# Forget gate steps that keep their filling, and an opening whose norm weight row is spread by a product with ones

## The chip, the cores and the metric

The kernel runs on one core of one Trainium2 chip. The metric is the device time of one execution in microseconds (us). TensorE (PE in the profile, PEld for its weight loads) multiplies, ScalarE (ACT) and VectorE (DVE) work on its results, GpSimd (POOL) does a few small operations and one kind of DMA, and SyncE (SP) issues nearly all DMAs.

## The reference, cut to what matters

`x` is 256 rows of 1024 numbers. Two layers of a first block come first (the change lies in them), then two layers of a second block (feed forward, mixing, cross attention, feed forward), which the change doesn't touch.

```python
def first_block(x, pre_norm, post_norm, w_in, ...):
    for layer in range(DEPTH):                      # 2
        h = rmsnorm(x, pre_norm[layer])
        proj = h @ w_in[layer]
        (hq, hf, hi, hz, nq, kc, vc, ks, vs, kw, vw, ng, nz) = jnp.split(proj, offsets, axis=-1)
        o_h = hgrn2_mixer(heads(hq), heads(hf), heads(hi), lower_bounds[layer]...)
        o_h = rmsnorm(o_h, ...) * jax.nn.silu(hz)
        o_n = nsa_mixer(...) * jax.nn.silu(nz)
        y = jnp.concatenate([o_h, o_n], axis=-1) @ w_out[layer]
        x = x + rmsnorm(y, post_norm[layer])
    return x
```

`hf` is the forget gate: its log sigmoid (in layer 1 with a lower bound) is summed along each chunk of 64 rows.

## The kernel before, in words

**Numbers in two parts.** A product of 32-bit numbers is made from three products of rounded parts: each weight piece (128x2048, 1 MB) is split by ACT into a high part (`split_high`, L2261) and by DVE into a low part (`split_low`, L2477). The activations are turned by TensorE (`turn`, L2023), then split by ACT (`turn_split`, L2278) and DVE (L2501). `tok` (L1968, L1972 for the weight's high part, L1978 for its low part) multiplies one weight piece with one tile of 128 rows, 12 products of 512 columns. `ch` (L1992, L1995, L1998) does 128 output columns of one piece for both tiles, 12 products of 256 columns.

**The plan.** A Python planner (`make_plan`) writes one list of steps, and each engine runs those that are its own in the order of the list. An engine's queue is strictly in order, so a step that waits holds back all behind it on its engine.

**Opening.** SP issues `load_ident`, `load_x` of tile 0, weight piece p0, `load_x` of tile 1, p1, p2, 17 small loads, p3, the constants, p4, p5 and `load_swap`. POOL issues a DMA (`gpre`, L2987) that copies the norm's weight row, 4 KB, to all 128 partitions, 512 KB. Both tiles are normed (`norm_squares` on ACT L2350, `norm_mean` on DVE L2565, `rstd` on POOL L2965, `norm_scale` on DVE L2573). The plan's order (`begin`, seam without `yb`) is: square tile 0, scale it, split_high p0, square tile 1, turn tile 0, both turn_splits of tile 0, scale tile 1, then the splits of p1, p2, p3 with their low parts. `mm_halves` then runs tile 0 over p0, p1, p2, p3, and then tile 1 over the same four: eight `tok`, tile 1 turned ahead of the fourth. A piece's slot comes free with its tile 1 product. `gT` is a small table of turned weights that `setup` (L1936) fills after the eight `tok`.

**The spread.** In each layer of the first block, `spread(plan, main, side)` mixes main steps (compress, the two attention groups `nsa(0)`, `nsa(1)`, and `recurrence`, one step of each in turn by `both`) with filling from `projections` and `out_early`, which is weight products for TensorE. After each main step the variable `ahead` falls by `plan.pace` (2.0, from the queries on 1.0, from the end of attention on 2.2) times 2400 units of planned TensorE work, and the side runs until it is positive again. A `ch` counts 3072 units, which is 1.28 paces of 2400; a `tok` counts 2.56. The second heads' projection `hgrn_qf(1)` runs inside this filling. It alternates eight `ch` of the query with the gate's steps (`softplus` on ACT for each half, `forget` on DVE for each half, L2742 to L2752, in layer 1 `bounded` L2758 to L2763, then `decay` L2770 and `log_key`: ACT L2425, DVE L2777), through `both`. Each gate step but the last cluster ends in `yield "rest"`, and at a rest `spread` stops filling and sets `ahead = 0`. The main steps beside it are those of attention: `scores` (PE L2032, DVE L2540 to L2547), `soft_exp` (ACT L2326), `nsa_gate` (DVE L2725 to L2730), `keys` (PE L2040, copied by ACT L2335 or DVE L2554) and `pv` (PE L2049). The first heads' `hgrn_qf(0)` runs outside `spread`, with nothing between; after it come `same` (PE L2130) and the level steps (L2141, L2152, L2805, L2812).

```python
            if step == "rest":
                ahead = 0
        yield
```

Of the kernel before, what the change touches and what calls it, by code (L numbers as in the profile page):

```python
# [12 lines left out]
ALU = mybir.AluOpType  # L13
# [3 lines left out]
P = 128  # L17
# [129 lines left out]
class Signals:  # L147


    def __init__(self, sem):  # L150
# [21 lines left out]
        self.x = [sem(f"s_x{t}") for t in range(2)]  # L172
# [159 lines left out]
def spread(plan, main, side):  # L332

    live, ahead = True, 0
    for more in main:
# [38 lines left out]
class Plan:  # L374
# [37 lines left out]
    def later(self, us, part):  # L412

        self.lag.append((self.work + us * 2400, part))
# [181 lines left out]
    def turn_pairs(self, name, src, need, h, t, scal=None, gains=None):  # L596
# [5 lines left out]
        for q, bank in enumerate(banks):  # L602
            self.split_bank(name, q, bank, h.pairs[q], t, ("turnp", name, q), scal,
                            None if gains is None else gains[:, 4 * q:4 * q + 4])
            h.made(t, q, name)

# [96 lines left out]
class Seam:  # L703
# [3 lines left out]
    def __init__(self, plan, name, gain_rows, yb=None, gsrc=None, half=False, norm=True):  # L707
# [4 lines left out]
        if norm:  # L712
# [3 lines left out]
    def turn_row(self, t):  # L716
# [3 lines left out]
        self.plan.turn_pairs(name, tmp.ap, [[("row", f"{self.name}.n{t}", i)] for i in range(2)], self.h, t)  # L720
        self.plan.U.give(tmp, ("turnp", name, 1))

    def steps(self, t):
# [17 lines left out]
        if self.norm:  # L741
            for self.row[t] in plan.norm(nn, x, plan.x_made[t], ("gpre", self.name), plan.m.gpre[:, :]):
                yield
# [43 lines left out]
def begin(plan, seam, make_jobs):  # L787
    if seam.yb is None:
        plan.split_next(True)
        steps = seam.steps(1)  # L790
        next(steps)
        seam.turn_row(0)
        for _ in steps:
            pass
        plan.hold = False
        plan.pump()
    else:
        if seam.h is None:
            seam.turn_row(0)
        seam.turn(1)  # L800
    plan.lead = LEAD
    jobs = make_jobs()
    yield from plan.mm_halves(jobs, seam.h, lambda: seam.turn_row(1))
# [3 lines left out]
def make_plan(A, m, order):  # L807
# [9 lines left out]
    plan.x_made = [[("x_in", t)] * 2 for t in range(2)]  # L817
    plan.gpost_used = plan.gpre_used = None
    do("load_ident")
    do("load_x", t=0, dst=plan.xt[0].ap)  # L820
# [72 lines left out]
    def first_layer(l, seam):  # L893
        w_in, w_out = A["w_in"][l], A["w_out"][l]
        N = f"a{l}"
        def jobs():
            return [(f"{N}.kv{br}", plan.weight(w_in, 0, 8, c0, 512), [B.take(), B.take()])
                    for br, c0 in enumerate((5632, 6144))]

        made = []  # L900
        h = yield from begin(plan, seam, lambda: made.extend(jobs()) or made)
        if l == 0:
            setup()
# [244 lines left out]
        def hgrn_qf(hg):  # L1148
# [5 lines left out]
            made_q, key = [], []  # L1154

            def gate_f():
                t2 = bounds = None
                if l == 1:
                    t2 = U.take()
                    bounds = [a[:, 4 * hg:4 * hg + 4] for a in (LNLB, LN1M, NEG_LNLB)]  # L1160
                yield "rest"
                for q, (b, pr) in enumerate(fb):
                    do("softplus", name=H, q=q, need=pr, bank=b, tl=tl, t2=t2, bounds=bounds)
                    yield "rest"
                for q, (b, pr) in enumerate(fb):
                    do("forget", name=H, q=q, bank=b, k_=k_, tl=tl, tc=tc, bounds=bounds)
                    B.give(b, ("logf", H, q))
                    yield "rest"
                if l == 1:
                    do("bounded", name=H, k_=k_, tl=tl, tc=tc, t2=t2, bounds=bounds)  # L1170
                    U.give(t2, ("bounded", H))
                do("decay", name=H, bb=bb, tc=tc, need=("bounded", H) if l else ("logf", H, 1))
                U.give(tl, ("decay", H))
                U.give(tc, ("decay", H))
                kk = U.take()
                do("log_key", name=H, sp=k_, kk=kk, bb=bb, need=("sp_bounded", H) if l else ("softplus_f", H, 1))
                key.append(kk)

            def query():
                for q, (b, pr) in enumerate((yield from proj_ch(f"{H}.q", 512 * hg, 512))):  # L1180
                    made_q.append(plan.copy(f"{H}.q{q}", [pr], q_.ap[:, q * 512:q * 512 + 512], b.ap, "act",
                                            q_.after))
                    B.give(b, made_q[-1])

# [1952 lines left out]
```

## Time and profile before

| | us |
|---|---|
| median of 3 runs | 2163.52 (2162.01 to 2165.08) |
| profiled execution, its own time | 2163.67 |
| its span in the trace | 2161.9 |
| TensorE busy | 2103.6 |
| VectorE busy | 1418.8 |
| ScalarE busy | 1051.7 |
| GpSimd busy | 110.1 |

The profiled execution lies 0.15 us above the median, and 1.8 us of its time lie outside the span. A view of the trace is read as start (us from the span's start), duration, engine, line of the kernel, what is written and read, and in brackets how long the engine stood idle before it and what ended that.

### The profile page before, as it was taken

The page shows a single profiled execution, that of the slowest core. Times are in us where ns is not written, and L with a number is a line of the kernel's source. Part 1 is how long each engine was busy: PE and PEld are TensorE (multiplying, and loading weights), DVE is VectorE, ACT ScalarE, POOL GpSimd, SP SyncE. Part 2 cuts the span into 40 slices and gives each one's busy share as a digit, 9 for nine tenths or more (in the row PEclk, how much of TensorE's full clock was granted, in tenths as well). Part 3 has the DMA queues.
Part 4 walks back from the last instruction along what each step waited for, and adds up shares of the span by engine and source line. Part 5 has one row for each costly group of instructions (what it writes and reads, how often), then busy time and mean ns, then how long its engine had stood idle before and what let it go on. Part 6 is the DMA issues. An engine that isn't in the chain of part 4 may idle for free.

```text
span 2161.9 us, 27716 instructions
## 1 busy us (share of the span) xinstructions
PE 2103.6 (97%) x11555; PEld 1804.1 (83%) x11555; DVE 1418.8 (66%) x1802; ACT 1051.7 (49%) x1520; POOL 110.1 (5%) x121
## 2 busy tenths in 40 slices
PE   7999999999899999999999999999999999999998
PEld 6989887988787888787888888888888878888887
DVE  4657866747777766665775666576666666755665
ACT  5444545534544644544544455455545454454543
POOL 0100200100011100000000000000100000000000
PEclk9999999999999999999999999999999999999999
DMA  7453235353234765445455455565645445554552
GB/s 278 121 196 118 84 131 176 121 191 130 78 130 150 243 208 172 150 148 165 169 185 183 136 196 189 184 212 184 214 149 180 138 160 173 192 175 147 180 191 98
DMA packets 193125, 357.76 MB, mean 165 GB/s; under 512 B 8364, under 2 KB 85352, under 8 KB 193000
## 3 DMA queue, kind: packets, MB, share of 16 engines
q1 hardware_dynamic: 190120, 345.51, 47.9%
q0 software_dynamic: 2880, 10.49, 1.5%
q8 instruction: 91, 1.49, 0.3%
q14 instruction: 34, 0.28, 0.0%
HBM read 354.92 MB, written 1.05 MB: 165 GB/s over the span
## 4 chain that ended last, share of the span: by engine, by line
PE 87%; DVE 8%; ACT 2%; issue 1%; DMA 1%; POOL 0%; DVEq 0%; SPq 0%; ACTq 0%
PE bank L1972 16%; PE bank L1978 16%; PE bank L1968 16%; PE bank L2010 12%; PE bank L2014 6%; DVE raw_r L2477 3%; PE bank L2032 3%; PE bank L2049 2%; PE bank L2152 2%; PE bank L2023 2%; PE bank L1992 2%; PE bank L1995 2%; PE bank L1998 2%; PE bank L2070 1%; PE bank L2040 1%
## 5 line engine op out<-in xcount | busy, mean ns | idle before, releaser
L2477 DVE TENSOR_TENSOR raw_r<-raw,high 128x2048 fp32r<-128x2048 f32 x304 | 686.3, 2272 | 84.4 <-ACT high L2261 83.3
L2261 ACT ACTIVATE high<-raw 128x2048 fp32r<-128x2048 f32 x304 | 575.1, 1896 | 246.5 <-PE bank L1978 195.9
L1968 PE MATMUL bank<-high,units_r 128*128 128x512 f32 (+1 forms) x1576 | 630.8, 400 | 7.0 <-ACT units_r L2278 7.0
L1972 PE MATMUL bank<-high,units_r 128*128 128x512 f32 (+1 forms) x1576 | 618.7, 393 | 14.7 <-DVE units_r L2501 12.0
L1978 PE MATMUL bank<-raw_r,units_r 128*128 128x512 f32 (+1 forms) x1576 | 424.6, 390 | 4.0 <-DVE raw_r L2477 4.0
L1972 PEld LDWEIGHTS bank<-high,units_r 128*128 128x128 f32 x1576 | 297.8, 189 | 79.7 <-DVE units_r L2501 16.5
L1968 PEld LDWEIGHTS bank<-high,units_r 128*128 128x128 f32 x1576 | 297.9, 189 | 69.0 <-issue 10.8
L1978 PEld LDWEIGHTS bank<-raw_r,units_r 128*128 128x128 f32 x1576 | 296.5, 188 | 68.1 <-DVE raw_r L2477 6.4
L2010 PE MATMUL bank<-units_r,high 128*128 128x512 f32 x1152 | 288.2, 392 | 0.3 <-DVE units L2833 0.3
L2010 PEld LDWEIGHTS bank<-units_r,high 128*128 128x128 f32 x1152 | 208.4, 189 | 38.7 <-issue 0.6
L2014 PEld LDWEIGHTS bank<-units_r,raw_r 128*128 128x128 f32 x1152 | 157.2, 190 | 11.2
L2014 PE MATMUL bank<-units_r,raw_r 128*128 128x256 f32 x1152 | 160.6, 282 | 0.0
L2833 DVE TENSOR_TENSOR units<-bank,units 128x256 f32<-128x256 f32 x144 | 60.3, 421 | 151.2 <-ACT units L2294 151.2
L2965 POOL TENSOR_TENSOR stat<-stat,halfs 128x1 f32<-128x1 f32 (+2 forms) x64 | 52.7, 825 | 1708.2 <-DVE stat L2586 895.8
L2294 ACT ACTIVATE units<-bank 128x256 f32<-128x256 f32 x144 | 54.2, 376 | 170.2 <-PE bank L2014 170.2
L2326 ACT ACTIVATE units<-units,stat 128x256 f32<-128x256 f32 (+2 forms) x176 | 74.0, 422 | 117.9 <-DVE stat L2547 117.6
L2278 ACT ACTIVATE units_r<-bank 128x512 fp32r<-128x512 f32 x92 | 49.7, 595 | 141.0 <-PE bank L2023 107.2
L1992 PE MATMUL bank<-units_r,high 128*128 128x256 f32 x448 | 117.2, 293 | 0.0
L1995 PE MATMUL bank<-units_r,high 128*128 128x256 f32 x448 | 114.0, 286 | 0.0
L2501 DVE TENSOR_TENSOR units_r<-bank,units_r 128x512 fp32r<-128x512 f32 x84 | 53.9, 684 | 55.8 <-ACT units_r L2278 55.8
L1995 PEld LDWEIGHTS bank<-units_r,high 128*128 128x128 f32 x448 | 87.4, 195 | 0.4
L1992 PEld LDWEIGHTS bank<-units_r,high 128*128 128x128 f32 x448 | 87.4, 195 | 0.5
(258 smaller groups left out, 2213.5 us busy)
## 6 DMA issues: line engine op xcount, KB each, us to landing
raw<-in_ffn_w_dram SPq DMA_DIRECT2D x132, 1024.0 KB, 5.1
raw<-in_w_in_dram SPq DMA_DIRECT2D x108, 1024.0 KB, 5.1
raw<-in_w_out_dram SPq DMA_DIRECT2D x24, 1024.0 KB, 4.9
raw<-in_cross_wkv_dram SPq DMA_DIRECT2D x16, 1024.0 KB, 5.1
raw<-in_w_branch_dram SPq DMA_DIRECT2D x12, 1024.0 KB, 4.9
raw<-in_cross_wq_dram SPq DMA_DIRECT2D x8, 1024.0 KB, 5.1
raw<-in_cross_wo_dram SPq DMA_DIRECT2D x8, 1024.0 KB, 4.8
raw<-in_w_in_dram SPq DMA_DIRECT2D x4, 832.0 KB, 4.6
```

The source lines that it names most:

```text
L1968: pe.matmul(o, h.high(k0 + k)[:, span], p.hi[k][:, cols], start=start and k == 0, stop=False, skip_group_check=True)
L1972: pe.matmul(o, h.low(k0 + k)[:, span], p.hi[k][:, cols], start=False, stop=False, skip_group_check=True)
L1978: product = pe.matmul(o, h.high(k0 + k)[:, span], p.lo[k][:, cols], start=False, stop=stop and k == p.k - 1, skip_group_check=True)
L1992: pe.matmul(o, w, h.high(k0 + k), start=first and k == 0 and c % 2 == 0, stop=False, skip_group_check=True)
L1995: pe.matmul(o, w, h.low(k0 + k), start=False, stop=False, skip_group_check=True)
L2010: pe.matmul(bank.ap.rearrange("p (a s) -> p a s", a=2), p.hi[k][:, c * P:c * P + P], h.whole(k, m.units_r), start=k == 0, stop=False, skip ...
L2014: product = pe.matmul(bank.ap[:, 0:256], p.lo[k][:, c * P:c * P + P], h.high(k), start=False, stop=k == p.k - 1, skip_group_check=True)
L2032: score = pe.matmul(bank.ap[:, i * L:i * L + L], left, right, start=j == 0, stop=j == steps - 1, skip_group_check=True)
L2261: done = act.activation(high, raw, ACT.Copy)
L2326: done = act.activation(p3[:, h, :], p3[:, h, :], ACT.Exp, bias=mx[:, h:h + 1], scale=1.0, accum_out=sm[:, h:h + 1])
L2477: done = dve.tensor_tensor(low, raw, high.bitcast(F32), ALU.subtract)
L2833: dve.tensor_tensor(dst, bank.ap[:, 0:256], dst, ALU.add).then_inc(*mark(s.vout, ("folded", name, c)))
```

## The change

**Filling.** In `spread` a rest now ends the filling after this main step, and `ahead` keeps its value. In `hgrn_qf` the gate's steps become nine (layer 0: six) single parts, each followed by a rest: `bounded` is cut into three phases, and `decay` and `log_key` each stand alone. The query's copies no longer wait for the end of the gate's list, and whichever comes last, key or query, makes the result known to the recurrence. `later` inserts by due time.

**Opening.** The weight row is fetched by SP in front of all else, 4 KB to one partition. POOL sets a row of ones, and two TensorE products (one row by 512 columns) spread it over 128 partitions into two PSUM banks, from which `norm_scale` of both tiles reads it. The POOL DMA of 512 KB is gone. x is loaded by halves, four DMAs with a semaphore each, and tile 0 of x now stands ahead of the identity. In the plan, tile 0 is turned, its first half split, then p0 split high and low, then its second half split, then tile 1 normed. Then each piece is used with both tiles before the next: p0 tile 0, turn tile 1, p1 tile 0, p0 tile 1, p1 tile 1, then p2 and p3 likewise.

```diff
-            if step == "rest":
-                ahead = 0
+            if step == "rest":
+                break
...
     if seam.yb is None:
-        plan.split_next(True)
-        steps = seam.steps(1)
-        next(steps)
-        seam.turn_row(0)
-        for _ in steps:
-            pass
-        plan.hold = False
-        plan.pump()
+        def first_piece():
+            plan.split_next(True)
+            plan.low_next()
+
+        seam.turn_row(0, first_piece)
+        for _ in seam.steps(1):
+            pass
+        plan.lead = LEAD
+        for i, (name, w, banks) in enumerate(make_jobs()):
+            for t in range(2):
+                for pi, (k0, p) in enumerate(w):
+                    if i == t == 0 and pi == len(w) - 1:
+                        seam.turn_row(1)
+                        plan.hold = False
+                    plan.tok(name, p, t, [banks[t]], seam.h, k0, pi == 0, pi == len(w) - 1)
+                    yield
+        return seam.h
...
+    do("load_gain", src=gain_rows.pop(0))
+    do("load_x", t=0, dst=plan.xt[0].ap)
     do("load_ident")
-    do("load_x", t=0, dst=plan.xt[0].ap)
...
+            parts = [(softplus, 0), (softplus, 1), (forget, 0), (forget, 1)]
+            parts += [(bounded, phase) for phase in range(3)] if l else []
+            parts += [(decay,), (log_key,)]
+
+            def gate_f():
+                yield "rest"
+                for part, *how in parts:
+                    part(*how)
+                    yield "rest"
...
+    def gain_row(banks, **_):
+        hold.wait_ge(*at(("ones",)))
+        hold.wait_ge(*at(("gain_in",)))
+        for i, b in enumerate(banks):
+            pe.matmul(b.ap, m.gT[0:1, 0:P], m.gpre[0:1, i * 512:i * 512 + 512], start=True, stop=True,
+                      skip_group_check=True).then_inc(*mark(s.turned, ("gain_row", i)))
+        hold.wait_ge(*at(("ident",)))
...
+    pool.memset(m.gT[0:1, 0:P], 1.0).then_inc(*mark(s.pstep, ("ones",)))
...
     def load_x(t, dst, **_):
-        sp.dma_start(dst, A["x"][0, t * P:(t + 1) * P, :]).then_inc(*mark(s.x[t], ("x_in", t), by=16))
+        for i in range(2):
+            sl = slice(i * 512, i * 512 + 512)
+            sp.dma_start(dst[:, sl], A["x"][0, t * P:(t + 1) * P, sl]).then_inc(
+                *mark(s.x[2 * t + i], ("x_in", t, i), by=16))
+
+    def load_gain(src, **_):
+        sp.dma_start(m.gpre[0:1, :], src).then_inc(*mark(s.gain, ("gain_in",), by=16))
```

## Rows read from the trace of the kernel before

**Rows 1.** Waits of TensorE over the span: engine line, releaser: us, times, longest.
```profile
PE bank L1972 <- DVE units_r L2501: 12.0, 11, 2.5
PE bank L2023 <- DVE units L2573: 8.3, 1, 8.3
```

**Rows 2.** Timeline of the opening, from the landing of x to the first products.
```profile
4.88 0.63 ACT L2350 ACTIVATE units<-units 128x512 f32<-128x512 f32 x1 [2.85 <-DMA units<-in_x_dram]
...
7.43 1.42 DVE L2573 SCALAR_TENSOR_TENSOR units<-units,stat,gpre 128x512 f32<-128x512 f32 x2 [1.02 <-DMA gpre<-in_pre_norm_dram]
...
8.32 1.94 PE L2023 MATMUL bank<-consts,units 128*128 128x128 f32 x8 [8.32 <-DVE units L2573]
...
9.71 1.91 ACT L2261 ACTIVATE high<-raw 128x2048 fp32r<-128x2048 f32 x1 [3.50 <-DMA raw<-in_w_in_dram]
...
12.75 1.06 ACT L2278 ACTIVATE units_r<-bank 128x512 fp32r<-128x512 f32 x2
...
13.47 0.77 PE L1968 MATMUL bank<-high,units_r 128*128 128x512 f32 x1 [3.21 <-ACT units_r L2278]
13.71 1.91 ACT L2261 ACTIVATE high<-raw 128x2048 fp32r<-128x2048 f32 x1
...
15.12 0.63 PE L1972 MATMUL bank<-high,units_r 128*128 128x512 f32 x1
...
15.38 1.41 DVE L2573 SCALAR_TENSOR_TENSOR units<-units,stat,gpre 128x512 f32<-128x512 f32 x2 [0.67 <-POOL stat L2965]
...
16.71 8.89 DVE L2477 TENSOR_TENSOR raw_r<-raw,high 128x2048 fp32r<-128x2048 f32 x4
...
19.05 2.08 PE L1978 MATMUL bank<-raw_r,units_r 128*128 128x512 f32 x4 [1.60 <-DVE raw_r L2477]
...
22.53 0.39 PE L1968 MATMUL bank<-high,units_r 128*128 128x512 f32 x1
```

**Rows 3.** Window: length, busy of PE, PEld, DVE, ACT, POOL; clock; DMA share, GB/s.
```profile
8.00:10.00 2.00, 1.68 (x8) 1.57 (x8) 0.84 (x2) 0.29 (x1) 0.00 (x0) 1.00 1.04 414
```

**Rows 4.** Chain of waits, start and duration: ends of two `tok`, `setup`, ends of two `ch`.
```profile
35.42 0.91 PE bank L1978 x4
38.14 0.91 PE bank L1978 x4
...
42.08 0.26 PE bank L1936
...
46.17 0.48 PE bank L1998 x4
47.61 0.48 PE bank L1998 x4
```

**Rows 5.** Timeline: `keys` behind the gate's steps, layer 0.
```profile
234.80 1.97 PE L2040 MATMUL bank<-consts,units 128*128 128x128 f32 x8 [3.54 <-DVE units L2730]
```

**Rows 6.** The same in layer 1.
```profile
565.16 1.97 PE L2040 MATMUL bank<-consts,units 128*128 128x128 f32 x8 [3.73 <-DVE units L2730]
...
581.12 2.41 PE L2049 MATMUL bank<-units 128*128 128x128 f32 x14 [2.97 <-DVE units L2554]
```

**Rows 7.** Windows behind the gaps, columns as in rows 3.
```profile
238.00:240.00 2.00, 2.00 (x12) 2.00 (x11) 1.93 (x5) 0.64 (x1) 0.00 (x0) 0.50 0.00 0
240.00:242.00 2.00, 2.00 (x16) 2.00 (x16) 1.97 (x2) 0.00 (x0) 0.00 (x0) 0.79 0.00 0
...
568.00:569.00 1.00, 1.00 (x8) 1.00 (x8) 1.00 (x3) 0.00 (x0) 0.00 (x0) 0.73 0.00 0
...
1234.00:1236.00 2.00, 2.00 (x7) 1.54 (x6) 1.90 (x5) 0.00 (x0) 0.55 (x1) 0.53 0.70 238
...
1972.00:1974.00 2.00, 1.67 (x7) 1.42 (x8) 2.00 (x5) 0.00 (x0) 0.39 (x1) 1.00 1.04 361
```

**Rows 8.** Timeline after the first heads' gate, layer 1: key, then `same`.
```profile
391.27 1.04 ACT L2425 ACTIVATE units<-units 128x1024 f32<-128x1024 f32 x1
...
395.49 2.05 PE L2130 MATMUL bank<-units 128*128 128x128 f32 x16 [0.69 <-ACT units L2288]
```

More of the change, by code:

```diff
@@ L170, in __init__ @@
         self.pstep = sem("s_pstep")
-        self.x = [sem(f"s_x{t}") for t in range(2)]
+        self.x = [sem(f"s_x{i}") for i in range(4)]
+        self.gain = sem("s_gain")
         self.const = sem("s_const")
@@ L412, in later @@
     def later(self, us, part):
-        self.lag.append((self.work + us * 2400, part))
+        at = self.work + us * 2400
+        i = sum(due <= at for due, _ in self.lag)
+        self.lag.insert(i, (at, part))
     def due(self, all_=False):
@@ L605, in turn_pairs @@
             h.made(t, q, name)
+            if between and q == 0:
+                between()
     def split_bank(self, name, q, bank, pair, t, need, scal=None, gains=None):
@@ L711, in __init__, with turn_row @@
             plan.do("gpost", name=name, src=gsrc, used=plan.gpost_used)
-        if norm:
+        self.gain = gain
+        if norm and not gain:
             plan.do("gpre", name=name, src=gain_rows.pop(0), used=plan.gpre_used)
         self.h = None
-    def turn_row(self, t):
+    def turn_row(self, t, between=None):
         if t == 0:
@@ L719, in turn_row @@
         tmp, name = self.row[t], f"{self.name}.h{t}"
-        self.plan.turn_pairs(name, tmp.ap, [[("row", f"{self.name}.n{t}", i)] for i in range(2)], self.h, t)
+        self.plan.turn_pairs(name, tmp.ap, [[("row", f"{self.name}.n{t}", i)] for i in range(2)], self.h, t,
+                             between=between)
         self.plan.U.give(tmp, ("turnp", name, 1))
@@ L741, in steps @@
         if self.norm:
-            for self.row[t] in plan.norm(nn, x, plan.x_made[t], ("gpre", self.name), plan.m.gpre[:, :]):
+            for self.row[t] in plan.norm(nn, x, plan.x_made[t], *(self.gain or ([("gpre", self.name)] * 2, plan.gpre))):
                 yield
@@ L895, in first_layer @@
         N = f"a{l}"
+        made = []
         def jobs():
[L897 to L901, printed above, removed]
+            for br, c0 in enumerate((5632, 6144)):
+                made.append((f"{N}.kv{br}", plan.weight(w_in, 0, 8, c0, 512), [B.take(), B.take()]))
+                yield made[-1]
+        h = yield from begin(plan, seam, jobs)
         if l == 0:
+            for b in g_banks:
+                B.give(b, ("row", "in.n1", 1))
             setup()
@@ L1154, in hgrn_qf, with softplus, forget, bounded @@
             made_q, key = [], []
[L1156 to L1170, printed above, removed]
+            t2 = bounds = None
+            if l == 1:
+                t2 = U.take()
+                bounds = [a[:, 4 * hg:4 * hg + 4] for a in (LNLB, LN1M, NEG_LNLB)]
+            def softplus(q):
+                do("softplus", name=H, q=q, need=fb[q][1], bank=fb[q][0], tl=tl, t2=t2, bounds=bounds)
+            def forget(q):
+                do("forget", name=H, q=q, bank=fb[q][0], k_=k_, tl=tl, tc=tc, bounds=bounds)
+                B.give(fb[q][0], ("logf", H, q))
+            def bounded(phase):
+                do("bounded", phase=phase, name=H, k_=k_, tl=tl, tc=tc, t2=t2, bounds=bounds)
+                if phase == 2:
                     U.give(t2, ("bounded", H))
+            def decay():
                 do("decay", name=H, bb=bb, tc=tc, need=("bounded", H) if l else ("logf", H, 1))
@@ L1177, in gate_f, with ready @@
                 key.append(kk)
+                ready()
+            def ready():
+                if key and len(made_q) == 2:
+                    st_["qf", hg] = (q_, k_, bb, key[0], made_q[-1], ("key", H), ("log_key", H))
             def query():
@@ L1906, in drive @@
                 return e.value
-    seam = Seam(plan, "in", gain_rows)
+    g_banks = [B.take(), B.take()]
+    do("gain_row", banks=g_banks)
+    seam = Seam(plan, "in", gain_rows, gain=([("gain_row", i) for i in range(2)], [b.ap for b in g_banks]))
     seam.turn(0)
```

50 lines of the change are left out of this document (27 added, 23 removed).

## The prediction

> **What bounds the kernel now.** I read the waits of TensorE first. It is busy for 2103.6 of 2161.9 us, so 58.3 us is all that an order of work can win, and the reader is to see how few waits make up much of it: 8.3 us in one piece ahead of the first turn and 12.0 us in eleven small ones [rows 1], and 7.3 us in two pieces ahead of `keys` [rows 5, 6]. The eleven lie nearly all at the seams, which the change leaves alone. The other two lie where the change works, so I read two timelines next, the opening and the stretch beside the gate's steps, and then the granted clock behind each gap.
>
> **Opening, what is on the path.** The time up to `setup` at 42.08 [rows 4] is made of a late start and a slow start. Tile 0 is squared from 4.88, and its scaling starts at 7.43, after a wait of 1.02 whose last releaser is the copied weight row [rows 2]. The turns end at 10.26. Their halves are split only at 12.75, because ACT's queue has split_high p0 (9.71 to 11.62, held by the weight's landing) and the squares of tile 1 in front. The first product starts at 13.47, and a 1.60 gap waits for p0's low part, which DVE does only from 16.71, behind the scaling of tile 1 [rows 2]. A product of 512 columns takes 0.63 at 15.12 and 0.39 at 22.53 [rows 2]. The granted clock reads 1.00 here all the while, but the durations show the lower level, 1.2 GHz, in the first stretch: 0.43 from product to product (512 columns at 1.2 GHz), against 2.72 for twelve, so 0.23, later [rows 4].
>
> **Opening, step by step after.** The weight row (4 KB) and half of x go first. POOL's 512 KB DMA is gone; its row of ones is one more tiny operation ahead of nothing. SP has three more issues (weight row, two second halves), so p0 and all behind it are issued later; no row here prices one, and I take 1 us for the three at most. The transfers queue up behind each other anyway, and half a megabyte less stands in them. The two spreading products run while x is still on its way; no row shows one, they lie between nothing (hidden before 4.88) and 1.7 us, twice the cold spacing of a 512-column product with a second pass, and even that ends before the turns. I take nothing.
> Scaling then starts at about 6.8 (between 6.2, all of the wait of 1.02 and a little of the squares saved by the first half of x, and 7.4 as now). The first turn is done about 1.9 us later at 8.7, its ACT half (0.53) at 9.2. Split_high p0 starts there if p0 has landed; it landed by 9.71 with the 512 KB beside it, and at the 414 GB/s of 8 to 10 us [rows 3] that much is 1.3 us, so 8.4 to 9.7. It ends at 11.1 (11.6 at the late end), and `tok` of p0 and tile 0, which needs only the first half and p0, starts there. DVE makes p0's low part (8.89 for four, so 2.2) right behind, at 13.3, before its products are due. Cold, twelve products at 0.43 end at 16.2. Tile 1: squares behind the second half's split, 11.7 to 13.0, mean and rstd 0.8 (before, 0.67 of DVE's wait for POOL and the mean), scaling 1.41, so 15.3; its turns fit behind 16.2 and take 1.0 warm, 1.9 cold. At 17.2 seven `tok` are left at 2.72 each [rows 4], 19.0 us, so `setup` comes at 36.2 instead of 42.08. Each piece now feeds TensorE for 5.4 us against 2.2 of DVE and 1.9 of ACT, so no split is late; p1 must be split by 17.2, and ACT took it up at 13.71 even before [rows 2]. The gain is 5.9. Bounds: 3.4 (p0 as late as now and the turns and one `tok` still cold) to 7.0.
>
> The Trainium skill, page "DMA: Bandwidth & Descriptors", "Anatomy of one DMA", speaks against halves: a DMA costs about 2.0 us fixed and then its bytes at 436 GB/s. By it a half of x issued at 1.66 lands at about 4.3, no later than the whole at 4.88 in the trace, so its fixed part hides behind the first half and the sum stays.
>
> **Filling, what the gaps are.** In layer 0 `keys` waits 3.54 us for DVE's `nsa_gate` [rows 5]. DVE has attention's scores, then a `forget`, and only then this `nsa_gate`; TensorE has one `ch` beside all that. In layer 1 the same place waits 3.73, and `pv` 16 us later waits 2.97 for a copy on DVE behind `bounded`, `decay` and `log_key` in one block [rows 6]. Each of these gaps lets the clock fall. In layer 0 it is at 0.50, the 1.2 GHz level, at 238 to 240 and ends within 240 to 242 (0.79, so at 240.8); the eight products of `keys` at 234.80 took 1.97, so it was low from there [rows 5, 7]: 6 us of half work, 3.0 lost. Behind 565.16 it ends at about 568.5 (0.73), 3.3 us, so 1.6 lost. Behind 581.12 I take the same 1.6; no row here is given for it, and 0 and 3.0 bound it.
>
> **Filling, step by step after.** A `ch` leaves `ahead` at +0.28 paces, the next main step at -0.72, and the gate step's rest wipes that out. Four such rests and a small one lose 2.9 paces of filling per layer, and a `ch` comes only every second main step. After the change the debt stays and each main step gets a gate step and a `ch`. Walking the list: between `scores` and the waiting `keys` there are now two `ch`, not one. DVE's order there (scores, forget, nsa_gate) is as before, since `forget` of the second half moves in front of `nsa_gate` where that of the first half was. So the gap is 3.54 less 1.44, the spacing of two `ch` [rows 4], 2.1 us; in layer 1 3.73 less 1.44, 2.3. In layer 1 the block on DVE is cut, two `tok` (5.4 us) come between `keys` and `pv`, and I find 0.4 left of 2.97, so 2.6 gained. Sum of gaps: 1.44 + 1.44 + 2.6 = 5.5.
> Costs: `log_key` of layer 1's first heads now stands behind the query's copies, so `same`, which waits 0.69 for these, waits for the key of 1.04 too [rows 8]: 1.0. The second heads' level steps now follow `keys` at one place without filling, 0.7, and near the end of layer 1 one level step loses its `tok`, 0.5. Together 2.2, bounds 0 and 5. Net of gaps 3.3.
> Clock: the two longest seam gaps, 2.5 each [rows 1], one ahead of 1233.6 and one ahead of 1972.3, tell what 2.1 and 2.3 may do. Behind the first the clock fell (0.53), behind the second it did not (1.00) [rows 7]; behind 2.97 and more it fell each time. I give 2.1 and 2.3 a chance of one third, and 0.4 none: 2.0 + 1.1 + 1.6 = 4.7, less a little, 4.4. Bounds 0 to 6.2.
> The Trainium skill, page "TensorE: Matmul & The Clock Gate", "HAM oscillation", says that too long an idle stretch throttles TensorE again, and its "Part 1" that the watch over it runs free of the program. By that rule, the pair at 2.5 agrees.
> These two gaps, shifted in time, may fall or not anew. The shift at the seams is worth 1.6 either way for each of the two; it stands in the range.
>
> **Is the pulled-forward filling missed later?** The walk says no. The second heads start four main steps earlier in layer 0 and three in layer 1, so fewer of their steps fall after attention's end, where a step draws 2.2 paces and not 1.0. That saves about the 2.9 paces that are no longer lost. The filling ends at the same main step as before, ahead of the last `hgrn_v`.
>
> **Sum.** 2163.67 of the profiled execution (0.15 above the median, which I drop) less 5.9, 3.3 and 4.4 is 2150.1.
>
> **Rivals.** (A) The opening works, the gate's gaps don't close: DVE is the engine that ends last there, a moved split_low (2.2) slips in front of `nsa_gate`, and the gaps and the low clock stay. 2163.67 - 5.9 + 0.5 = 2158. For it: in layer 1 DVE is nearly full beside the gate; against: my walk has the split ahead of the scores. (B) The gate works, the opening doesn't: p0 or p1 lands as late as now and all is late behind ACT. 3.4 or less of the opening, so 2154 to 2156. (C) Slower: the filling drawn early is missed in the level steps, where each step without a `tok` shows a chain of DVE, ACT and DVE of about 2.5 us. It decides the sign when four steps in each layer stand bare (20 us, against 13.6), and gives 2170. Against it: the walk ends the filling at the same step. (D) The change does nothing that can be seen: the opening's gain is given back by a wait for the constants or the small loads at `setup`, and (A) too. 2162.
>
> **How the numbers follow.** Forecast 0.63, A 0.17, B 0.11, C 0.04, D 0.05. Within 0.2% means 4.3 us, about what a measurement can tell, so above 2159.3 counts as the same; a quarter of A reaches there. Faster 0.87, same 0.09, slower 0.04. The range runs from 2144 (opening 7.0, clock kept everywhere, 6.2, costs near 1) to 2158, which takes in B and the better half of A.
>
> **What would show it.** `setup` (L1936) between 35 and 39; first L1968 at 11 and no wait of L1978 behind it; no POOL DMA of the weight row in the opening. Waits of L2040 on L2730 two at about 2.2, that of L2049 on L2554 under 1. Granted clock 1.00 around 235 and 575. `same` of layer 1 waiting 1.7 on ACT. I am wrong if the gaps at L2040 are over 3 or new waits on L2477 or L2812 over 2 us appear in the level steps.

## The result, and the profile after

| | before | after |
|---|---|---|
| median, us | 2163.14 (2162.01 to 2165.08, 4 runs) | 2150.53 (2149.81 to 2151.60, 4 runs) |
| span of the profiled execution | 2161.9 | 2148.2 |
| TensorE busy | 2103.6 | 2099.2 |
| VectorE, ScalarE, GpSimd busy | 1418.8, 1051.7, 110.1 | 1417.2, 1051.1, 102.2 |

The ratio is 0.9941, 95% interval 0.9924 to 0.9958: faster by 12.6 us. Forecast were 2150.1 and "faster", a gain of 13.6. The total is right to half a microsecond; three of its terms are not, and they cancel.

TensorE's waits in the changed kernel (engine, line, releaser: us, times, longest). The first row answers [rows 1], the second [rows 5, 6]; L2021, L2072, L2089, L2190 and L2179 are the old L1972, L2023, L2040, L2141 and L2130.

```profile
PE bank L2021 <- DVE units_r L2550: 12.1, 11, 2.5
PE bank L2089 <- DVE units L2779: 4.4, 2, 2.3
...
PE bank L2017 <- ACT high L2310: 2.9, 1, 2.9
...
PE bank L2190 <- DVE units L2865: 2.6, 2, 1.9
...
PE bank L1976 <- DMA gpre<-in_pre_norm_dram: 2.3, 1, 2.3
PE bank L2179 <- issue: 1.7, 1, 1.7
...
PE bank L2072 <- DVE units L2622: 1.3, 1, 1.3
```

The seams' 12 us stay. The 7.3 us ahead of `keys` are 4.4. New are 2.9 for the first piece, 1.9 ahead of `across` (L2190) and 1.7 ahead of `same` (L2179).

Timeline of the opening after, which answers [rows 2] (columns as there):

```profile
2.27 3.75 PE L1976 MATMUL bank<-gpre,gT 1*128 1x512 f32 x4 [2.27 <-DMA gpre<-in_pre_norm_dram]
...
4.22 0.63 ACT L2399 ACTIVATE units<-units 128x512 f32<-128x512 f32 x1 [2.19 <-DMA units<-in_x_dram]
...
6.45 1.41 DVE L2622 SCALAR_TENSOR_TENSOR units<-units,stat,bank 128x512 f32<-128x512 f32 x2 [0.68 <-POOL stat L3019]
...
7.34 1.94 PE L2072 MATMUL bank<-consts,units 128*128 128x128 f32 x8 [1.32 <-DVE units L2622]
8.46 0.60 ACT L2327 ACTIVATE units_r<-bank 128x512 fp32r<-128x512 f32 x1 [2.89 <-PE bank L2072]
...
10.27 1.91 ACT L2310 ACTIVATE high<-raw 128x2048 fp32r<-128x2048 f32 x1 [1.21 <-DMA raw<-in_w_in_dram]
...
12.23 0.80 PE L2017 MATMUL bank<-high,units_r 128*128 128x512 f32 x1 [2.95 <-ACT high L2310]
...
15.75 1.10 PE L2027 MATMUL bank<-raw_r,units_r 128*128 128x512 f32 x4
16.68 1.27 PE L2072 MATMUL bank<-consts,units 128*128 128x128 f32 x8
```

Squares, scaling and turns come earlier, as forecast. Then ScalarE, done with the turns' half, waits 1.21 for the first piece. That piece now ends last. By the chain of waits `setup` stands at 37.3 where it stood at 42.08 [rows 4].

The gaps after, in order of time: two `keys` (L2089), which answer [rows 5, 6], and between them `across` and `same`, the latter answering the wait in [rows 8].

```profile
231.41 1.09 PE L2089 MATMUL bank<-consts,units 128*128 128x128 f32 x8 [2.11 <-DVE units L2779]
...
257.03 1.14 PE L2190 MATMUL bank<-units 128*128 128x128 f32 x8 [1.85 <-DVE units L2865]
...
390.49 1.69 PE L2179 MATMUL bank<-units 128*128 128x128 f32 x13 [1.68 <-issue]
...
562.39 1.09 PE L2089 MATMUL bank<-consts,units 128*128 128x128 f32 x8 [2.30 <-DVE units L2779]
```

And the windows behind the first, second and fourth and behind the seam gap (columns as in rows 3; compare [rows 7]):

```profile
232.00:234.00 2.00, 2.00 (x19) 2.00 (x18) 1.97 (x2) 1.90 (x3) 0.00 (x0) 1.00 0.00 0
258.00:260.00 2.00, 2.00 (x12) 2.00 (x11) 0.09 (x1) 1.79 (x4) 1.10 (x1) 0.50 0.27 109
260.00:262.00 2.00, 2.00 (x11) 1.92 (x11) 0.39 (x1) 2.00 (x2) 0.34 (x1) 0.64 0.03 8
...
565.00:567.00 2.00, 2.00 (x20) 2.00 (x19) 1.93 (x5) 0.92 (x1) 0.00 (x0) 1.00 0.00 0
1222.00:1224.00 2.00, 2.00 (x10) 1.62 (x10) 1.90 (x5) 0.00 (x0) 0.55 (x1) 1.00 0.80 273
```

The clock stays at 1.00 behind 2.11 and 2.30 and behind the seam gap of 2.44, and falls to 0.50 behind 1.85, which is shorter than all three.

### The profile page after: what moved, and what is told of

Its sections match the earlier page's. It is cut to its first block, busy times and chain, and to the rows that moved or that the text cites. A ratio compares the mean times of both kernels' runs of the same rounds, so it can differ in the third digit from the quotient of the medians.

```text
span 2148.2 us, 27730 instructions
## 1 busy us (share of the span) xinstructions
PE 2099.2 (98%) x11559; PEld 1799.1 (84%) x11559; DVE 1417.2 (66%) x1801; ACT 1051.1 (49%) x1519; POOL 102.2 (5%) x121
## 3 DMA queue, kind: packets, MB, share of 16 engines
HBM read 354.40 MB, written 1.05 MB: 165 GB/s over the span
## 4 chain that ended last, share of the span: by engine, by line
PE 88%; DVE 7%; ACT 3%; DMA 1%; issue 1%; POOL 0%; SPq 0%; DVEq 0%; ACTq 0%
PE bank L2021 16%; PE bank L2017 16%; PE bank L2027 16%; PE bank L2059 12%; PE bank L2063 6%; PE bank L2081 3%; DVE raw_r L2526 3%; PE bank L2201 2%; PE bank L2047 2%; PE bank L2041 2%; PE bank L2044 2%; PE bank L2098 2%; PE bank L2072 2%; PE bank L2119 1%; PE bank L2089 1%; DMA raw<-in_w_in_dram 1%
## 5 line engine op out<-in xcount | busy, mean ns | idle before, releaser
L2526 DVE TENSOR_TENSOR raw_r<-raw,high 128x2048 fp32r<-128x2048 f32 (+1 forms) x305 | 689.6, 2275 | 84.3 <-ACT high L2310 83.2
L2310 ACT ACTIVATE high<-raw 128x2048 fp32r<-128x2048 f32 (+1 forms) x305 | 577.0, 1896 | 243.2 <-PE bank L2027 192.3
L2017 PE MATMUL bank<-high,units_r 128*128 128x512 f32 x1584 | 632.3, 399 | 6.9 <-ACT units_r L2327 3.9
L2021 PE MATMUL bank<-high,units_r 128*128 128x512 f32 x1584 | 619.9, 391 | 14.7 <-DVE units_r L2550 12.1
L2027 PE MATMUL bank<-raw_r,units_r 128*128 128x512 f32 x1584 | 425.2, 389 | 2.4 <-DVE raw_r L2526 2.4
L2021 PEld LDWEIGHTS bank<-high,units_r 128*128 128x128 f32 x1584 | 298.4, 188 | 79.3 <-DVE units_r L2550 16.2
L2041 PE MATMUL bank<-units_r,high 128*128 128x256 f32 x448 | 114.6, 288 | 0.0
L2044 PE MATMUL bank<-units_r,high 128*128 128x256 f32 x448 | 112.1, 283 | 0.0
```

Of the source, the lines that this page charges most:

```text
L2017: pe.matmul(o, h.high(k0 + k)[:, span], p.hi[k][:, cols], start=start and k == 0, stop=False, skip_group_check=True)
L2021: pe.matmul(o, h.low(k0 + k)[:, span], p.hi[k][:, cols], start=False, stop=False, skip_group_check=True)
L2027: product = pe.matmul(o, h.high(k0 + k)[:, span], p.lo[k][:, cols], start=False, stop=stop and k == p.k - 1, skip_group_check=True)
L2041: pe.matmul(o, w, h.high(k0 + k), start=first and k == 0 and c % 2 == 0, stop=False, skip_group_check=True)
L2044: pe.matmul(o, w, h.low(k0 + k), start=False, stop=False, skip_group_check=True)
L2310: done = act.activation(high, raw, ACT.Copy)
```

## The experiments

Each run's landmarks (us) tell where it gained: the first `same`, the first product behind layer 0's end, the same for layer 1, the product behind the seam gap of 2.4, and the span. The last column counts the gaps behind which the granted clock fell after the opening, without the fall at the very end that every trace has. Each row is one profiled execution; that of the opening alone is the slowest of its eight runs, that of the filling alone the slowest of its six.

| run | `same` | layer 0 end | layer 1 end | seam | span | falls |
|---|---|---|---|---|---|---|
| before | 66.05 | 327.23 | 661.25 | 1233.61 | 2161.9 | 4 |
| after | 61.30 | 321.23 | 649.17 | 1221.71 | 2148.2 | 1 |
| opening only | 62.35 | 323.24 | 657.30 | 1229.66 | 2157.8 | 4 |
| filling only | 66.20 | 327.95 | 656.98 | 1229.43 | 2156.0 | 3 |
| debt kept | 61.73 | 320.15 | 653.47 | 1225.87 | 2154.0 | 3 |
| steps cut | 61.80 | 321.74 | 656.66 | 1229.09 | 2155.7 | 3 |
| level_mul early | 62.07 | 317.07 | 644.65 | 1216.99 | 2143.5 | 0 |
| + later parts whole | 61.23 | 314.71 | 641.69 | 1213.97 | 2142.1 | 1 |
| identity by POOL | 60.48 | 318.58 | 647.25 | 1219.73 | 2147.8 | 2 |
| p1 behind p0 | 60.81 | 320.49 | 649.28 | 1221.85 | 2151.7 | 4 |
| half MB back | 62.38 | 323.74 | 651.44 | 1223.91 | 2150.4 | 2 |
| old piece order | 62.20 | 322.02 | 649.81 | 1222.35 | 2148.9 | 1 |
| x whole | 62.22 | 323.76 | 652.50 | 1225.02 | 2154.8 | 5 |
| all three | 60.99 | 314.82 | 642.20 | 1214.66 | 2142.8 | 1 |

### Each half of the change alone

The changed kernel with `spread` and `hgrn_qf` of before; `later` stays as changed:

```diff
             if step == "rest":
-                break
+                ahead = 0
...
-            parts = [(softplus, 0), (softplus, 1), (forget, 0), (forget, 1)]
```

> The changed kernel with the filling part undone (the gate's steps whole, the debt dropped at a rest). Theory (the two parts add up): setup still at about 37.3 us, 4.7 earlier than before; the gaps of keys near 230 and 560 are 3.5 and 3.7 again and that of pv near 576 is 3.0, each with the granted clock at 0.5 behind it; the wait of 1.85 at the second heads' first level step is gone back to about 0.7. By the difference of the two traces the filling is worth 1.3 us in layer 0 and 6.0 in layer 1, so the span is 2148.2 + 7.3 = 2155.5, plus 1.7 if the clock falls behind the seam gap near 1229, time about 2157 to 2159. Rival (the filling's gain is a matter of where the clock happens to fall, not of the gaps): the gaps are back but the clock behind them is at 1.00 in two of the three, and the span is 2152 or less.

Measured: 2157.26 (2155.34 to 2159.60), ratio 0.9977 (0.9966 to 0.9988). Its gaps are those of before again (3.55, 3.73, 3.01), each with the clock at 0.50 behind it, and `same` of layer 1 waits 0.69.

The kernel before with the changed `spread` and `hgrn_qf`; `later` and the opening are those of before. Part of its edit, against the changed kernel:

```diff
-    do("load_gain", src=gain_rows.pop(0))
-    do("load_x", t=0, dst=plan.xt[0].ap)
     do("load_ident")
+    do("load_x", t=0, dst=plan.xt[0].ap)
...
-        seam.turn_row(0, first_piece)
+        plan.split_next(True)
+        steps = seam.steps(1)
```

> The kernel before with only the filling part. Theory: setup at 42.1 as before, gaps of keys 2.1 and 2.3 with the clock at 1.00 behind them, no gap of 3 us at pv, the wait at the second heads' first level step in layer 0 at about 1.9. Span 2161.9 less 7.3, 2154.6, or 1.7 less where the seam gap near 1226 keeps its clock; time 2154 to 2156.5. Rival (the gap of 1.9 and its low clock in layer 0 came from the opening's shift): layer 0 then gains 3 us or more instead of 1.3.

Measured: 2156.15 (2154.79 to 2157.77), ratio 0.9970 (0.9959 to 0.9982), with the gaps of the changed kernel to the hundredth: 2.11, 1.85, 1.68, 2.30. The product of both ratios is 0.9947, against 0.9941 for both at once: the parts add up, and what `later` does on its own is not seen in either. Layer 0, from `same` to its end, takes 261.8 where it took 261.2, so it gains nothing without the opening's shift either, against the rival. But the clock behind equal gaps was another. Behind 2.11 it fell here, as these windows of this run show (columns as in rows 3), and it did not in the changed kernel:

```profile
238.00:240.00 2.00, 2.00 (x12) 2.00 (x11) 1.97 (x3) 2.00 (x2) 0.00 (x0) 0.50 0.00 0
240.00:242.00 2.00, 2.00 (x14) 2.00 (x14) 2.00 (x2) 0.70 (x2) 0.00 (x0) 0.70 0.00 0
```

### The filling's two edits apart

The debt is kept, but the gate's parts stay as they were, `bounded`, `decay` and `log_key` in one block, and the result again waits for both lists, key and query:

```diff
-            parts = [(softplus, 0), (softplus, 1), (forget, 0), (forget, 1)]
-            parts += [(bounded, phase) for phase in range(3)] if l else []
-            parts += [(decay,), (log_key,)]
+                if l == 1:
+                    do("bounded", name=H, k_=k_, tl=tl, tc=tc, t2=t2, bounds=bounds)
```

> The changed kernel, but the gate's steps stay whole (bounded, decay and log_key in one block); only the debt is kept at a rest. Theory: keeping the debt is what puts the second block of columns between scores and keys, so both gaps of keys are about 2.1 and 2.3 as in the changed kernel. What cutting the block buys is the gap at pv in layer 1: some of the 3.0 stays (1 to 3 us). Rival: the cut is what helps all three, and the gaps of keys are over 3.

Measured: 2155.78, one run. Both keys gaps fell below what I had expected, to 0.67 and 0.86, since three `ch` now stand between `scores` and `keys`. In layer 1 the block of `bounded`, `decay` and `log_key` stayed in one piece and a wait of 5.08, more than the 1 to 3 expected, stands at the `pv` right behind `keys`, one earlier than the one that waited 2.97 before (this run's timeline):

```profile
568.52 3.78 PE L2080 MATMUL bank<-units 128*128 128x128 f32 x16 [5.08 <-DVE units L2585]
```

The other way round, steps cut and debt dropped:

```diff
-                break
+                ahead = 0
```

> The changed kernel with its cut steps, but the debt dropped at each rest as before. Theory: only one block of columns stands between scores and keys, so the gaps of keys are about 3.5 and 3.7 again with the low clock behind them, and as there are more rests now more filling is lost; pv in layer 1 waits less than 3.0, since the block is cut. Span at least 4 us over the changed kernel's 2148.2. Rival: cutting alone closes the gaps, span within 2 us of 2148.2.

Measured: 2157.49, one run. The keys gaps are back at 3.55 and 3.73, the `pv` gap is gone, and a level step of layer 1 waits 2.01. The gap of 1.85 at `across` comes with the debt too: it stands in the run before and is 0.90 here. So the kept debt fills `keys` and the cut block frees `pv`; neither does the other's work. And the cut has a price that I had not seen: the rests that it adds, two in layer 0 and five in layer 1, eat up filling that the keys gap could have used (2.11 where 0.67 is to be had).

### The gap at `across`

```diff
             level_exp(0)
             level_from(1)
+            level_mul(0)
             yield
...
-                if li == 0:
-                    level_mul(0)
```

> The changed kernel with layer 0's level_mul emitted one main step earlier; nothing else differs. Theory (TensorE's new 1.85 us gap at `across` in layer 0 is the DVE queue: split_low, nsa_cat and the copy of keys stand in front of level_mul, 0.9 us late): with level_mul ahead of them the gap near 257 us falls to 0.5 or less, the granted clock stays at 1.00 behind it, and landmarks after it come 2.5 to 3.5 us earlier than in the changed kernel (seam gap 343.0 to about 340): span 2145 to 2146. Rival (the gap is the planner's order of PE work, the wait is ready only when the filling's copies are): the gap stays at 1.5 to 2, only its waited-on instruction changes, and the span stays within 0.5 us of 2148.2, or the copy of keys now comes 0.9 us later and the keys gap grows from 2.1 to 3.0 with the clock at 0.5 behind it: 2150.

Measured: 2145.53 (2145.32 to 2146.88), ratio 0.9924 (0.9909 to 0.9939). In the changed kernel DVE does a split_low, a step of attention and the copy of `keys` ahead of level_mul (L2865), and TensorE stands behind all of them (timeline of DVE):

```profile
250.95 2.29 DVE L2526 TENSOR_TENSOR raw_r<-raw,high 128x2048 fp32r<-128x2048 f32 x1
...
253.15 0.68 DVE L2784 TENSOR_TENSOR units<-bank,units 128x512 f32<-128x512 f32 x1
...
255.21 0.69 DVE L2603 COPY units<-bank 128x512 f32<-128x512 f32 x1 [1.38 <-PE bank L2089]
255.82 1.66 DVE L2865 TENSOR_TENSOR units<-units 128x512 f32<-128x512 f32 x2
```

With level_mul ahead of the split, `across` (here L2189) starts right behind `keys` (timeline of this run):

```profile
250.49 0.68 DVE L2864 TENSOR_TENSOR units<-units 128x512 f32<-128x512 f32 x1
...
251.09 2.28 DVE L2525 TENSOR_TENSOR raw_r<-raw,high 128x2048 fp32r<-128x2048 f32 x1
...
253.69 1.04 PE L2088 MATMUL bank<-consts,units 128*128 128x128 f32 x8
254.56 1.06 PE L2189 MATMUL bank<-units 128*128 128x128 f32 x8
```

The theory holds: from the first `keys` to the end of layer 0 it takes 86.1 where the changed kernel takes 89.8. Of these 3.7, the run with the identity on POOL, which has the gap of 1.85 but kept its clock behind it (88.2), gives 1.6 to the clock and 2.1 to the gap.

### The later parts of the gate without a rest

```diff
-                    yield "rest"
+                    yield "rest" if part in (softplus, forget) else 0
```

> As the run before it, and the forget gate's later parts (bounded, decay, log_key) keep DVE's block cut as in the change but no longer ask for the rest of a step's filling; only softplus and forget keep it. Theory (the keys gap of 2.1 and 2.3 us is one chunk of filling short, since the filling is eaten up by parts which need no cover): three chunks stand between scores and keys, so the two keys gaps are 0.7 and 0.9 us, no 3 us gap at the pv products, and the span is 2142 to 2145. Rival (what the later parts give up shows elsewhere: the filling ends later, so a DVE block stands in front of another tile): a gap of 2.5 us or more turns up at the pv products or in the level steps, clock at 0.5 behind it, and the span is 2147 to 2150.

This edit stands on top of the one before it. Measured: 2143.89 (2143.65 to 2145.10), ratio 0.9917 (0.9900 to 0.9933). Its timeline at the two `keys` and at `pv` (L2097):

```profile
230.07 1.09 PE L2088 MATMUL bank<-consts,units 128*128 128x128 f32 x8 [0.67 <-DVE units L2778]
...
555.51 1.09 PE L2088 MATMUL bank<-consts,units 128*128 128x128 f32 x8 [0.85 <-DVE units L2778]
...
571.16 1.83 PE L2097 MATMUL bank<-units 128*128 128x128 f32 x14 [0.64 <-DVE units L2602]
```

Both keys gaps are short and no long wait comes back at `pv`, as the theory had it. Up to the end of layer 1 it is 3.0 us ahead of the run before it, of which 0.84 were there at the first `same` and are not the edit's: 2.1 us are, less than the 2.9 by which the keys gaps shrank, since `pv` now waits 0.64. The seam gap then cost it the clock (0.50), which that run had kept, so the spans differ by 1.4.

### What sets the first piece's landing

The identity's DMA started by POOL:

```diff
-        sp.dma_start(m.consts[:, 0:P], A["consts"][:, 0:P])
+        pool.dma_start(m.consts[:, 0:P], src)
```

> The changed kernel with the identity's DMA started by POOL, so SP starts the first piece of x one issue (about 0.4 us) earlier: 2.1 where the changed kernel has 2.50. Theory (the first piece lands at 10.25 because it is issued 0.84 us later than before and shares the queues' bandwidth with what stands behind it): it lands 0.4 us earlier, at 9.8, ScalarE's split of it starts with it and the first token product at about 11.8 (12.23 in the changed kernel); span 2147.8. Rival (its landing is set by the bytes on the way, not by its issue): landing stays at 10.1 to 10.4, first token product at 12.2.

The second piece issued when the first has landed:

```diff
+        if p.i == 1:
+            hold.wait_ge(*at(("raw", 0)))
         sp.dma_start(dst, src)
```

> The changed kernel with SP waiting for the first piece's landing before it issues the second and what follows. Theory (the first piece's 7.7 us from issue to landing are stretched by the pieces behind it, which share the 16 DMA engines): it lands 1 us or more earlier, at 9.2 or before, the first token product starts at 11.2, and the second piece, issued at 9.2, lands 4 us or more later than in the changed kernel, so that TensorE waits 2 to 4 us at the second piece's products; span 2150 to 2152. Rival (pieces are served in the order they are issued, and those behind cost the first nothing): it lands at 10.0 to 10.4 as before, and only the later pieces are late: span 2151 to 2154.

The 512 KB of before given back, into a buffer that nobody reads yet:

```diff
+        pool.dma_start(m.gpost[:, :], src.partition_broadcast(P))
```

> The changed kernel with a 512 KB DMA given back: POOL copies the 4 KB row to 128 partitions of a buffer that is not used yet, as early as before; nobody waits for it in the opening. Theory of the prediction (the bytes stand in the queues ahead of the first piece, 512 KB at 414 GB/s are 1.3 us): ScalarE's split of the first piece starts at 11.5 where the changed kernel has 10.27, the first token product at 13.4 (12.23), setup at 38.5 (37.33). Rival (from the issue to the landing the first piece took 8.05 us with the 512 KB beside it and 7.77 without, so these bytes cost it 0.3 us): split at 10.4 to 10.7, first token product at 12.4 to 12.7, setup at 37.4 to 37.8.

x by whole tiles:

```diff
-        for i in range(2):
-            sp.dma_start(dst[:, sl], A["x"][0, t * P:(t + 1) * P, sl])
+        sp.dma_start(dst, A["x"][0, t * P:(t + 1) * P, :])
```

> The changed kernel with x loaded by whole tiles (two DMAs, not four), so the first piece is issued one issue (0.43 us) earlier, at 2.07. Theory (as in the run with the identity on POOL, what is issued ahead of the first piece delays it by its issue and a bit): ScalarE's split of it starts 0.4 to 0.8 earlier than 10.27, and since the squares of tile 0 start 0.2 to 0.6 later than 4.22 with cover to spare before that split, the first token product comes at 11.5 to 11.9 and setup at 36.5 to 36.9. Rival (halves pay by the early start of squares, scaling and turns): scaling starts at 7.1 or later (6.45 with halves), the ScalarE half of the turns ends after the piece's landing, and setup is at 37.3 or later.

Measured, one run each (2149.58, 2153.51, 2152.23 and 2156.60 us), from the timelines:

| run | scaling | p0 issued | split of p0 starts | first `tok` | products at 1.2 GHz until |
|---|---|---|---|---|---|
| after | 6.45 | 2.50 | 10.27 | 12.23 | about 15.5 |
| opening only | 6.35 | 2.50 | 10.29 | 12.26 | about 17.5 |
| identity by POOL | 6.92 | 2.03 | 9.43 | 11.38 | about 14.3 |
| p1 behind p0 | 6.23 | 2.51 | 9.67 | 11.63 | about 14.9 |
| half MB back | 8.21 | 2.51 | 10.72 | 12.68 | about 17.9 |
| x whole | 7.08 | 2.04 | 10.22 | 12.18 | about 17.5 |

The level is read from the products: 0.43 from one to the next is the lower one, 0.23 the higher, as in the prediction; the granted clock reads 1.00 throughout this stretch.

How much a single trace says here shows in the seven that load their opening alike, the changed kernel, the opening alone, debt kept, steps cut, level_mul early, later parts whole and the old piece order. In them p0 is issued at 2.50 or 2.51, but its split starts anywhere from 9.87 to 10.76, and the first `tok` from 11.83 to 12.72.

With x whole, p0 is issued 0.46 earlier and its split starts at 10.22, inside that range: no gain of the earlier issue is seen. Not issuing the second piece until the first has landed brings the split to 9.67, only 0.2 ahead of the earliest of the seven and less than the 1 us expected, so that what stands behind a transfer stretches it is not shown. The late second piece cost nothing (setup at 36.8), against theory and rival. Moving the 64 KB identity to POOL is the one edit that stands clear: the split starts at 9.43, and at 9.49 in the run with all three below, without any wait for the piece, 0.4 or more ahead of the earliest of the seven. Why 64 KB weigh that much isn't settled.

Half a megabyte given back hit x first, whose second half came late, by the timeline of that run:

```profile
6.61 0.63 ACT L2400 ACTIVATE units<-units 128x512 f32<-128x512 f32 x1 [1.51 <-DMA units<-in_x_dram]
```

Scaling starts 1.76 later, and of that 0.45 reaches the first `tok`, since TensorE waited for the piece anyway. The rival's split and first `tok` are right, its reason (bytes beside the piece) is not: the piece had landed by 10.72, when ScalarE came to it. `setup` comes at 38.4, later than the rival's 37.8, since the lower level lasted longer. Of the 1.3 us that I took off the piece's landing for these bytes at most 0.45 are there against the changed kernel, and at most 0.9 against the earliest of the seven.

Halves of x start the squares at 4.22, the whole at 4.88 as before [rows 2], which moves scaling by 0.63; none of it reaches the first `tok`. With x whole `setup` comes at 38.2, as the rival had it, but not for its reason: the turns' half ends at 9.70, ahead of the piece, and the lower level lasts until 17.5. The halves' second squares need no wait, so the second half had landed by 4.86, when the whole had. The Trainium skill, page "DMA: Bandwidth & Descriptors", "Anatomy of one DMA", gives each DMA that GpSimd issues a fixed part; x is issued by SyncE, but by that rule, as weighed in the prediction, the trace agrees: the second half, issued behind the first, was there at most 0.7 later, so its fixed part hid behind the first.

### The order of pieces alone

```diff
-        for i, (name, w, banks) in enumerate(make_jobs()):
-            for t in range(2):
+        plan.hold = False
+        plan.pump()
+        yield from plan.mm_halves(list(make_jobs()), seam.h, lambda: seam.turn_row(1))
```

> The changed kernel with its opening's products in the order of before: tile 0 over all four pieces, then tile 1. Theory (the pieces come slower than one tile eats them, 2.7 us a product warm, so each piece must feed both tiles): TensorE waits for the second to fourth piece's split or low part by 1 to 3 us in all, and setup comes at 38.5 to 40 where the changed kernel has 37.33. Rival (the earlier start alone makes the gain, the order is worth nothing): no wait over 0.5 us at the products of pieces two to four, setup at 37.0 to 37.8.

Measured: 2150.71, one run, setup at 38.2. One wait for the second piece's low part is nearly all that the old order costs (timeline of this run):

```profile
19.41 1.21 PE L2022 MATMUL bank<-raw_r,units_r 128*128 128x512 f32 x4 [0.74 <-DVE raw_r L2521]
```

`same` is 0.90 later than in the changed kernel, 0.74 of it this wait, with the clock up at the same place in both. (The other traces with this opening lie up to 1.05 later as well, but none has this wait.) It lies between theory and rival: the pieces keep pace but for the second.

### The best of it

Level_mul early, later parts whole, identity by POOL:

> The run with the later parts whole plus the identity on POOL: level_mul early, later parts of the gate without a rest, first piece issued earlier. Theory (the three add up): keys gaps of 0.7 and 0.9 us, no gap of 1.85 at `across`, setup at 36.4; span 2141.2, or 2139.6 if the clock stays up behind the seam gap of 2.4 near 1212, median 2142 to 2143.5. Rival (the earlier opening is given back, since the seams' waits and the clock's falls are luck of timing): span 2142 to 2145, no faster than the run without it (2142.1).

Measured: 2144.12 (2143.46 to 2144.55), ratio 0.9915 (0.9902 to 0.9929). No faster than without the identity's move (0.9917): the rival. The first `same` is 0.24 earlier, and by the first `keys` (230.17 against 230.07) this is given back, to a wait of 0.72 at L2200 near 149 that the other run does not have over 0.6. By the ratios both are some 5 us faster than the change itself, though the intervals overlap a little with its own (0.9924 to 0.9958).

## Why the prediction came out right

**Opening: right in mechanism, mis-sized in one term.** Forecast was a gain of 5.9, measured are 4.7 at `same`, and 3.7 to 4.8 in the six traces with this same opening. Scaling at 6.8 (6.45) and ScalarE's half done at 9.2 (9.06) held. SP's three more issues cost 1.34 at p1 where I took 1; the two of them ahead of p0 cost 0.84. The step that failed is the landing of p0, "8.4 to 9.7": it is 10.24, later than before, by the chain of waits after:

```profile
2.50 7.74 DMA raw<-in_w_in_dram
```

Before, the same chain has:

```profile
1.66 8.03 DMA raw<-in_w_in_dram
```

So the piece was issued 0.84 later and took 0.29 less: my working took 1.3 off the landing for the 512 KB and never added the later issue, which it had priced one sentence earlier. That moved the first `tok` from 11.1 to 12.23. A second term gave part of it back: I had all twelve first products at the lower level (5.1 us); the higher one came after eight (4.45). With the opening alone it did not, and `setup` stood at 38.4 instead of 37.3, which shows that this microsecond is the clock's and not the change's. The spreading products took 3.75 us where my bound was 1.7: each showed as two instructions. They were done at 6.02, only 0.4 ahead of scaling, which reads them and not the turns, and scaling waited for POOL, so nothing of it is on the path.

**Keys and pv: right.** The gaps of 2.1 and 2.3 are 2.11 and 2.30. For `pv`, 0.4 was forecast to be left of 2.97. Nothing is left at that `pv`, but another one, ahead of `keys`, which had no wait before, now waits 0.82 for ScalarE (at 553.18). 5.0 us gained where I had 5.5.

**Costs of the filling: one right, one missed.** `same` waits 1.68 (1.7 forecast). "0.7 at one place without filling" is 1.85, because I counted TensorE's missing filling and not what stands in DVE's queue: the walk followed the list for `nsa_gate`, but not for level_mul. A level step of layer 1 waits 0.75, but at the same place it waited 0.52 before, and another wait of 0.52 is gone (405.25 before); the forecast 0.5 near the layer's end isn't there. Together 2.6 for 2.2, counting what each adds.

**The clock: the expectation right, its composition not.** I had 4.4 for falls that disappear. Gone are the three of before (6.2 by the windows of [rows 7] and my 1.6, for which the trace of before does show a fall of 4 us behind 581.12, from 582 to 586), and at the seam of 1222 it stayed up (1.65: from there to the next seam 187.0 where before took 188.6). A new fall behind 1.85 takes 1.6. That is 6.2, 1.8 more than forecast, and it pays for the gap that I missed. The seam gap's fall I had left in the range, not in the sum.

**Sum.** 4.7 + 2.4 + 6.2 is 13.3 of the span's 13.7; the rest lies in waits too small to list. Forecast were 5.9, 3.3 and 4.4: the opening and the net of the gaps came out 2.1 short, the clock 1.8 over. That these cancel to half a microsecond is luck, the clock's above all. (The range's low end of 2144 also needs the 1.6 of a seam gap; the three terms named for it make 2146.0.)

**Rivals.** (A) is refuted by the gaps, (C) by the level steps, of which only `across` with its 1.85 stands newly bare. (B) was half true: p0 is late, yet the opening still gains 4.7. For (D) nothing waits at `setup`.

## What to carry over

Where a wait is cut, walk the queue of every engine that feeds the next product, not only of the one that was late: one operation emitted one step earlier was worth another 3.7 us here, 1.6 of it clock. A rule meant to protect a chain (stop filling here) should cover only the steps which need that: taking it off the later parts was worth 2.1 us. When a transfer is awaited, add up what is issued ahead of it, small loads too; a kernel's first load may be late even though less is moved in all.

## What the runs showed of the hardware

Gaps of a length had no fixed effect on the granted clock. Over 14 traces, gaps at one place with the clock at 0.50 behind them:

| gap, us | place | fell |
|---|---|---|
| 2.97 to 5.08 | `keys`, `pv` | 9 of 9 |
| 2.43 to 2.47 | seam near 1222 | 7 of 14 |
| 2.43 to 2.47 | seam near 1959 | 3 of 14 |
| 2.30 | `keys`, layer 1 | 4 of 8 |
| 2.11 | `keys`, layer 0 | 3 of 8 |
| 2.01 | level step, layer 1 | 1 of 1 |
| 1.85 | `across` | 7 of 8 |
| 1.68 | `same`, layer 1 | 0 of 11 |
| 1.35 to 1.39 | seam near 1410 | 0 of 14 |

The one time that the clock stayed up behind 1.85 is the run with the identity by POOL, whose order there is that of the changed kernel (window of that run, columns as in rows 3):

```profile
258.00:260.00 2.00, 2.00 (x15) 1.78 (x14) 1.05 (x2) 2.00 (x4) 1.32 (x2) 1.00 0.03 8
```

A fall cost 1.0 to 1.1 behind 2.30, 1.5 behind 2.11 and 1.6 at `across` and the seams, by the time from landmark to landmark in runs that fell and runs that did not. These prices explain the single runs: with x whole the clock fell behind all five, which are 7.3 - 1.6 = 5.7 us more than in the changed kernel, and with 0.9 from the opening that makes 2154.8, the measured span. Nor is it fixed for one kernel: the eight runs of the opening alone lie between 2155.34, at a mean granted clock of 0.998, and 2159.60, at 0.995. So a single run of one of these kernels says little under 3 us. The Trainium skill, page "TensorE: Matmul & The Clock Gate", "HAM oscillation", says that too long an idle stretch throttles TensorE again; by it alone the clock should fall behind 2.11 whenever it does behind 1.85, and in three traces (the changed kernel, p1 behind p0, old piece order) it fell behind 1.85 only. What else decides, such as the work ahead of the gap, no run here tells apart.
